# Sixteen gate products in an attention stage: two in every three turns of its first part, none in its second

## The reference, cut to what matters

```python
z = jnp.einsum('bld,dlf->blf', u, w_in)             # w_in: 1024 x 6656
qa, ka, va, qb, kb, vb, ga, gb = jnp.split(z, cut, axis=-1)   # ga, gb: 1024 columns each
# branch a: 8 heads; each has two score maps (64 wide) with a distance bias
w  = softmax(q1 k1^T / 8 - slope * dist) - lam * softmax(q2 k2^T / 8 - slope * dist)
oa = w @ v
# branch b: 8 query heads over 2 key/value heads (128 wide), one score map each
ob = softmax(q k^T / sqrt(128)) @ v
ya = oa @ w_branch_a
yb = ob @ w_branch_b
merged = sigmoid(ga) * ya + sigmoid(gb) * yb
h = h + merged @ w_out
```

## Time and profile before

| | |
|---|---|
| median of 3 runs | 1372.9 us (1371.93 to 1375.32) |
| the profiled execution's own time | 1375.32 us |
| its span in the trace | 1373.5 us |
| TensorE busy | 1286.6 us, 94% of the span |
| attention stage, first scores to start of branch_b | 855.48 to 997.68 us of the span |
| mean granted TensorE clock | 0.969 of full speed |

### The profile page before, as it was taken

How to read it: one execution, slowest core, us unless ns; L and a number is a source line. 1 busy time by engine, 2 the same in 40 slices (tenths; PEclk the granted TensorE clock), 3 DMA queues, 4 the chain that set the end, 5 groups by cost and what they waited for, 6 DMA issues and landing times.

```text
span 1373.5 us, 25936 instructions
## 1 busy us (share of the span) xinstructions
PE 1286.6 (94%) x11356; PEld 949.4 (69%) x11356; DVE 543.0 (40%) x1188; ACT 339.9 (25%) x868; POOL 136.7 (10%) x207
## 2 busy tenths in 40 slices
PE   6999998999987899999989999999999959999996
PEld 2435888899976788888878887656677744445433
DVE  1256234343434599992040641674252150111113
ACT  2434243333221222110011211455431112101101
POOL 0002254455200000120000000000000010000000
PEclk9999999999998999999999999999999959999998
DMA  9600002221126243434343333211022376999992
GB/s 395 282 0 32 2 33 67 93 95 65 65 93 248 99 175 131 177 107 171 123 150 127 120 124 141 102 62 62 17 109 85 131 336 252 420 427 430 427 427 96
DMA packets 18544, 223.08 MB, mean 162 GB/s; under 512 B 2112, under 2 KB 3264, under 8 KB 3968
## 3 DMA queue, kind: packets, MB, share of 16 engines
q1 hardware_dynamic: 18032, 220.05, 41.0%
q0 software_dynamic: 256, 1.06, 0.3%
q10 hardware_dynamic: 144, 0.31, 0.1%
HBM read 220.37 MB, written 1.05 MB: 161 GB/s over the span
## 4 chain that ended last, share of the span: by engine, by line
PE 91%; DVE 3%; DMA 2%; ACT 2%; issue 1%; SPq 0%; ACTq 0%; DVEq 0%
PE ps L597 37%; PE ps L718 13%; PE ps L1135 8%; PE ps L945 6%; PE ps L1004 5%; PE ps L1179 4%; PE ps L1146 2%; PE ps L1050 2%; DMA mem<-weights 2%; PE ps L1116 2%; PE ps L1021 2%; PE ps L696 1%; PE ps L792 1%; PE ps L1035 1%; ACT mem L1444 1%
## 5 line engine op out<-in xcount | busy, mean ns | idle before, releaser
L597 PE MATMUL ps<-mem 128*128 128x256 f32 (+2 forms) x2096 | 521.5, 406 | 19.6 <-DVE mem L1745 8.3
L597 PEld LDWEIGHTS ps<-mem 128*128 128x128 f32 x2096 | 399.3, 192 | 130.9 <-issue 50.5
L718 PE MATMUL ps<-mem 64*64 64x64 f32 (+1 forms) x5664 | 185.5, 223 | 4.0 <-issue 4.0
L718 PEld LDWEIGHTS ps<-mem 64*64 64x64 f32 x5664 | 178.6, 137 | 14.6 <-issue 14.2
L1774 DVE SCALAR_TENSOR_TENSOR mem<-ps,mem 128x189 f32<-128x189 f32 (+2 forms) x352 | 148.3, 431 | 14.8 <-ACT mem L1390 3.9
L1135 PE MATMUL ps<-mem 128*64 128x512 f32 x512 | 111.6, 592 | 0.5 <-ACT mem L1511 0.5
L1135 PEld LDWEIGHTS ps<-mem 128*64 128x64 f32 x512 | 37.3, 137 | 72.9 <-issue 72.2
L1999 DVE TENSOR_TENSOR mem<-ps,mem 128x512 f32<-128x512 f32 x8 | 5.5, 693 | 187.3 <-PE ps L1135 187.3
L945 PE MATMUL ps<-mem 128*128 128x256 f32 x352 | 77.0, 378 | 0.0
L945 PEld LDWEIGHTS ps<-mem 128*128 128x128 f32 x352 | 66.5, 189 | 9.7
L1242 ACT ACTIVATE mem<-ps 128x256 f32<-128x256 f32 x128 | 49.2, 384 | 83.0 <-PE ps L718 80.4
(11 more groups left out here) (252 smaller groups left out, 1235.0 us busy)
## 6 DMA issues: line engine op xcount, KB each, us to landing
mem<-experts SPq DMA_DIRECT2D x48, 2048.0 KB, 17.4
mem<-weights SPq DMA_DIRECT2D x44, 2048.0 KB, 7.8
mem<-late_ada SPq DMA_DIRECT2D x16, 1024.0 KB, 5.1
mem<-weights SPq DMA_DIRECT2D x3, 1536.0 KB, 6.6
mem<-tokens SPq DMA_DIRECT2D x1, 2048.0 KB, 12.3
mem<-consts SPq DMA_DIRECT2D x1, 1504.0 KB, 23.5
out<-mem SPq DMA_DIRECT2D x1, 1024.0 KB, 4.8
mem<-consts POOLq DMA_DIRECT2D x1, 776.0 KB, 5.4
```

The costliest lines, as they stand in the source:

```text
L597: last = mm(bank(j % banks)[:, 0:nn], w[:, kc, c * P:(c + 1) * P], rr(kc), start=kc == 0, stop=kc == KD - 1)
L718: last = mm(out[hp, j], lhs[hp, j], rhs[hp, j], start=i == 0, stop=i == len(terms) - 1)
```

## The change

The table `GATE_TURNS` goes away. The 16 gate chunks now sit in the turns n < 24 with n % 3 equal to 1 or 2: two for each head of branch a, none in branch b. Turns 1, 2, 4, 5, 7, 8, 11, 14, 17, 20 and 23 keep a chunk; turns 10, 13, 16, 19 and 22 get one, and turns 26, 29, 32, 35 and 38 lose theirs. The banks follow from the chunk's number (even: 7, odd: 6), and the waits are written for the new order.

```diff
--- before.py
+++ after.py
@@ -487,16 +487,8 @@
         def attended_bank(hd):
             return 6 if hd < AH else 6 + hd % 2
 
-        GATE_TURNS = sorted([1, 4, 7] + list(range(2, 39, 3)))
-
         def gate_bank(j):
-            return 7 if GATE_TURNS[j] % 3 == 1 else 6
-
-        def gates_until(n):
-            return sum(at < n for at in GATE_TURNS)
-
-        def attended_until(n):
-            return sum(3 * hd + 6 < n for hd in range(AH)) + sum(2 * (30 + 3 * p < n) for p in range(BH // 2))
+            return 7 - j % 2
 
         def free_bank(engine, name, n, banks=4):
             if n >= banks:
@@ -997,8 +989,8 @@
                     have_block(pe, b)
                 if j >= 2:
                     pe.wait_ge(S("proj2_taken"), 36 + j - 1)
-                if gate_bank(j) == 6 and attended_until(GATE_TURNS[j]) >= 1:
-                    pe.wait_ge(S("attended_kept"), attended_until(GATE_TURNS[j]))
+                if j >= 5 and j % 2:
+                    pe.wait_ge(S("attended_kept"), j // 2 - 1)
                 w, c = block_view(b), j % 4
                 for kc in range(KD):
                     last = mm(bank(gate_bank(j))[:, 0:L], w[:, kc, c * P:(c + 1) * P], u[:, kc, :], start=kc == 0, stop=kc == KD - 1)
@@ -1041,8 +1033,10 @@
                 for m in range(un.maps):
                     hd = un.out_head + m
                     pe.wait_ge(S("weights_kept"), 2 * (un.first_map + m + 1))
-                    if attended_bank(hd) == 6 or hd == AH + 1:
-                        pe.wait_ge(S("proj2_taken"), 36 + gates_until(n + 4))
+                    if hd == AH + 1:
+                        pe.wait_ge(S("proj2_taken"), 52)
+                    elif hd < AH:
+                        pe.wait_ge(S("proj2_taken"), 36 + min(2 * (hd + 2), 16))
                     if hd >= 1 and hd != AH + 1:
                         pe.wait_ge(S("attended_kept"), hd if hd <= AH else hd - 1)
                     e = un.head if un.diff else 8 + un.head // 4
@@ -1054,8 +1048,8 @@
             for n in range(len(units) + 4):
                 if n < len(units):
                     scores(n)
-                if n in GATE_TURNS:
-                    gate_chunk(GATE_TURNS.index(n))
+                if n < 24 and n % 3:
+                    gate_chunk(2 * (n // 3) + n % 3 - 1)
                 if 3 <= n <= len(units) + 2:
                     turn_weights(n - 3)
                 if n >= 4 and units[n - 4].tile == 2:
@@ -1472,8 +1466,8 @@
                 A(ga[:, j, :] if j < 8 else gb[:, j - 8, :], bank(gate_bank(j))[:, 0:L], ACT.Copy).then_inc(S("proj2_taken"), 1)
 
             for n in range(len(units) + 4):
-                if n - 1 in GATE_TURNS:
-                    keep_gate(GATE_TURNS.index(n - 1))
+                if 2 <= n < 26 and n % 3 != 1:
+                    keep_gate(2 * ((n - 1) // 3) + (n - 1) % 3 - 1)
                 if n < len(units):
                     exponentials(n)
                 if 3 <= n <= len(units) + 2:
```

## The result

| | before | changed |
|---|---|---|
| median of 4 runs | 1372.41 us (1368.91 to 1375.32) | 1384.6 us (1374.85 to 1386.88) |
| ratio, with its 95% interval | | 1.0114 (1.0081 to 1.0147) |
| profiled execution, span | 1373.5 us | 1382.1 us |

The change is slower by 1.1%, 11 to 20 us, and not by the 5.7 us that I forecast. The single executions scatter over 12 us, those of the kernel before over 6. In all, the record holds 37 executions of the changed kernel, from 1374.85 to 1394.82 us with a median of 1387.7, while those of the kernel before lie between 1367.0 and 1375.9 us wherever it was run.

A forecast was written before the change was run, and what follows sets the result against it. The prediction took TensorE, 94% busy, as the bound, with a ScalarE copy chain behind it in branch b. It summed +18.6 - 12.9 = +5.7 us onto 1372.9, giving 1378.6 us, range 1375.0 to 1383.0.

The forecast's parts named there:

- Five chunks into branch a, +18.6: Turns 10, 13, 16, 19 and 22 each gain a chunk costing 3.72 us of pass time, +18.60 us in all.
- The bubble of 0.6 us: TensorE's idle time in each branch a pass, after the second turn's chunk, claimed to stay unfilled by an added chunk.
- the row with two chunks: Earlier profile's branch a window holding two chunks: 13.09 us, TensorE busy 12.50, so its idle time remains.
- Five chunks out of branch b, -12.9: Turn 26 gives back 2.5 us, turns 29, 32 and 35 2.19 each, turn 38 3.8: -12.9 us.
- The chain: In branch b, transposes wait for ScalarE's copy of the previous unit's weights; 1.69 of a chunk's 3.88 us becomes idle.
- 10.5 us (turn 27 to 36): Expected profile sign: branch b passes of 10.5 us, with TensorE idle about 2.0 us in each.
- the term of 2.19: Time each chunk removed from turns 29, 32 and 35 gives back, shrinking a pass from 12.67 to 10.48 us.
- The rest: Rewritten waits, load order, chunk 12's weights and everything after attention: claimed to add no cost and no gain.
- The clock: Rival: emptier branch b passes let TensorE's clock fall, giving 1381.6 us; chance 0.12. The main sum included no clock cost.
- A fall of about 7 us at half speed leaves about 3 us of the work undone: Clock rival's pricing for the new branch b passes: 3 us added to the forecast, 1381.6 us; chance 0.12.

The follow-up runs named there:

- the kernel with the fitted filling: Changed kernel plus unused matmuls that fit TensorE's waits in turns 26, 29, 32 and 35 to 38: 1375.87 us, ratio 1.0033.
- the other profile: The changed kernel run again unaltered, beside the kernel before: median 1387.04 us, ratio 1.0106; its profiled execution was the shortest.
- the kernel with five filled waits: Kernel before, chunks unmoved, plus unused matmuls in five TensorE waits outside attention: 1359.81 us, ratio 0.9924.

## Why the prediction was wrong

**Five chunks into branch a, +18.6.** Right: +18.64. The bubble of 0.6 us stayed in each pass, as the row with two chunks had said.

**Five chunks out of branch b, -12.9.** Right: -12.97 with the clock up. By turn of the moved chunk, from the windows of the kernel with the fitted filling against the earlier trace rows: 26: 2.54 (forecast 2.5), 29, 32 and 35: 2.18 each (2.19), and 38: 3.92 (3.8). The chain was the one named, as ScalarE's timeline of the changed kernel shows, where the copy of the weights ends at 962.26 and the exponentials start 0.53 us later (forecast 0.52). The wait before the transposes is not put down to that copy by the profile, as I had said it would be, but to VectorE; the times given with the result show that it is ScalarE's all the same. And "10.5 us (turn 27 to 36)" was too coarse: the first of the three passes was 10.91 us before and not 12.67, so the term of 2.19 makes it 8.7, and 8.73 was measured with the clock up.

```profile
962.01 0.25 ACT L1454 ACTIVATE mem<-ps 16x128 f32<-16x128 f32 x1
962.79 0.48 ACT L1438 ACTIVATE mem<-ps,mem 16x272 f32<-16x272 f32 x1 [0.53 <-PE ps L1027]
```

**The rest.** Right: chunk 12's weights were there in time, and no new wait of a gate chunk showed.

**The clock.** Here it failed. The sum put the clock at nothing, and the step that was to cover it was "A fall of about 7 us at half speed leaves about 3 us of the work undone" with its chance of 0.12. That rival had the right place and mechanism. Its size and its frequency were wrong. In size: the profile has falls of 3.4 and 20.5 us. The stretch from turn 24 to the product took 54.72 us and not 47.33, so 7.4 us, and the first 16 matmuls after it 6.58 and not 3.95, 2.6 more: 10.0 us, where I had priced 3 (and 7 us at half speed are 3.5). In frequency: I counted one fall in eight executions. The changed kernel opens three waits of 1.39 us in a row, the last with one of 1.42 us behind it, and in both of its profiles at least one brought the clock down. I had also seen that my emptiest 2 us (0.5 us busy, and 0.51 was measured) lay between a row that was followed by a fall and one that wasn't; with three such places, a chance of one eighth for all of them together had nothing to rest on. With the clock's case priced at 10 us the range would have reached 1389.

5.7 + 10.0 = 15.7 us, and the ratio says 15.6. That the two agree to 0.1 us is luck: the first is from one execution, and the ratio's interval is 11 to 20 us. The executions themselves differ by the falls that they happen to have; in the other profile the clock cost 1.6 us in the stretch (48.92 against 47.33).

**The forecast's direction** was right: slower. The part that was worked out from rows alone held to 0.1 us in the profiles, but it is 5.7 of 15.6 us.

What stays open is why the second fall lasted 20.5 us. TensorE was busy 2.00 of 2 us in most of it, as in the window of 1006 above, and in other places of these profiles the clock was back after 3.4 to 10 us of such work.

## What to carry to other kernels

A piece of independent TensorE work between dependent steps has two values: the time that it hides, and the clock that it holds up. Moving it away costs both, and the second can be the larger: here 5.7 us for the five chunks against some 10 us for the clock, in the profiled execution. Where TensorE must wait and no real work is at hand, a few matmuls without a use that fit the wait can be worth their place; count how long one takes first, since too many lengthen the chain. And take several executions before judging such a kernel: two of the same one differed by whether the clock fell.

## What the runs showed of the hardware

The clock's fall is what I hadn't expected in this size. A wait of 1.4 us, in 2 us with 0.6 us of work, was followed by half the clock in one execution and not in another that did the same work to 0.01 us. In the kernel with five filled waits the clock fell in the middle of the router's matmuls, 2.4 us behind a wait of only 1.21 us. Nor had I expected a fall of 20.5 us under nearly dense work. The Trainium skill, page "TensorE: Matmul & The Clock Gate" (HAM oscillation — how this bites in real kernels), describes a loop that waits in every pass and pays for the clock in every pass. The trace agrees as far as the place goes, since the falls begin in the waits of the passes; but here not every pass pays, and one fall outlasted two passes.
